# A third buffer pair for the experts' weights, memory lent between stages, and a shared term added on TensorE

## What is computed

```python
def channel_sublayer(x, shift, scale, gate, w_router, e_bias, w1, w3, w2, ws1, ws3, ws2, ln_g, ln_b):
    u = modulate(x, shift, scale)
    B, S, D = u.shape
    h = u.reshape(B * S, D)
    idx, wts = route(h, w_router, e_bias)
    y = (jax.nn.silu(h @ ws1) * (h @ ws3)) @ ws2 + routed_experts(h, idx, wts, w1, w3, w2)
    return post_norm(x, gate * y.reshape(B, S, D), ln_g, ln_b)
```

## Time and profile before

| what | value |
|---|---|
| median of three runs | 1322.1 us (1322.06 to 1329.15) |
| the profiled execution | 1323.07 us, of which the span 1321.3 us |
| mean granted TensorE clock | 0.917 |
| PE, DVE, ACT, POOL busy | 78%, 32%, 18%, 17% |
| read and written | 329.15 MB, 29.52 MB, 271 GB/s over the span |

### The profile page before, as it was taken

How to read it: one execution, slowest core, us unless ns; L and a number is a source line. 1 busy time by engine, 2 the same in 40 slices (tenths; PEclk the granted TensorE clock), 3 DMA queues, 4 the chain that set the end, 5 groups by cost and what they waited for, 6 DMA issues and landing times.

```text
span 1321.3 us, 23547 instructions
## 1 busy us (share of the span) xinstructions
PE 1033.8 (78%) x8385; PEld 657.7 (50%) x8386; DVE 427.7 (32%) x815; ACT 239.2 (18%) x478; POOL 218.1 (17%) x361
## 2 busy tenths in 40 slices
PE   4899899986576699983787788877877878766865
PEld 3888788875565344542344444444433444433432
DVE  4523324338843113874411111111111121101118
ACT  3222212336455000110110101010100111100100
POOL 0002102000100000201222222222231223212211
PEclk9899999996799799997799889899898998978988
DMA  9587666521063793075689699987999988899955
GB/s 350 173 298 256 223 236 216 184 95 48 1 226 112 274 272 115 32 301 201 215 291 386 229 382 395 370 326 272 408 375 387 328 303 299 308 398 404 396 220 216
DMA packets 97912, 347.52 MB, mean 263 GB/s; under 512 B 15057, under 2 KB 20225, under 8 KB 73146
## 3 DMA queue, kind: packets, MB, share of 16 engines
q1 hardware_dynamic: 81258, 311.56, 63.7%
q0 software_dynamic: 13856, 30.13, 6.9%
q10 hardware_dynamic: 2736, 4.98, 1.0%
HBM read 329.15 MB, written 29.52 MB: 271 GB/s over the span
## 4 chain that ended last, share of the span: by engine, by line
PE 27%; DMA 16%; issue 6%; DVE 2%; SPq 1%; ACT 0%; POOL 0%; POOLq 0%; DVEq 0%; ACTq 0%
PE PS L1771 8%; DMA hT<-h_rows,ixo 7%; DMA W<-w 7%; PE PS L1786 6%; PE PS L1802 4%; PE PS L1827 4%; PE PS L1841 2%; PE PS L1777 1%; DMA vec<-ln_b 1%; PE PS L1759 1%; PE PS L1817 1%; DVE hido L1893 0%; PE PS L1794 0%; DVE hid L1888 0%; DMA W<-expert_rows 0%
## 5 line engine op out<-in xcount | busy, mean ns | idle before, releaser
L1771 PE MATMUL PS<-W,XT 128*32 128x256 f32 x2048 | 130.0, 410 | 48.5 <-DMA W<-w 26.5
L1786 PE MATMUL PS<-W,XTo 128*64 128x256 f32 x1216 | 139.5, 381 | 0.0
L1771 PEld LDWEIGHTS PS<-W,XT 128*32 128x32 f32 x2048 | 80.1, 118 | 114.8 <-issue 90.6
L1786 PEld LDWEIGHTS PS<-W,XTo 128*64 128x64 f32 x1216 | 93.2, 137 | 44.0 <-issue 10.6
L1802 PE MATMUL PS<-W,hidTo 128*64 128x512 f32 x304 | 90.7, 722 | 16.3 <-DVE hidTo L1896 10.7
L431 DVE TENSOR_TENSOR w_lo<-raw,w_hi 128x2048 fp32r<-128x2048 f32 x26 | 59.5, 2288 | 126.1 <-ACT w_hi L371 126.1
L305 PE MATMUL PS<-w_hi,u_hi 128*128 128x512 f32 x240 | 94.4, 393 | 1.7 <-DVE w_lo L431 1.7
L305 PE MATMUL PS<-w_hi,u_lo 128*128 128x512 f32 x240 | 93.5, 389 | 0.0
L305 PE MATMUL PS<-w_lo,u_hi 128*128 128x512 f32 x240 | 93.4, 389 | 0.0
L1827 PE MATMUL PS<-W,hidT 128*32 128x512 f32 x512 | 72.1, 677 | 26.3 <-issue 24.3
L1856 ACT ACTIVATE sg<-PS 64x256 f32<-64x256 f32 x32 | 12.1, 378 | 346.9 <-PE PS L1771 346.9
(11 more groups left out here) (338 smaller groups left out, 1497.8 us busy)
## 6 DMA issues: line engine op xcount, KB each, us to landing
W<-w SPq DMA_DIRECT2D x192, 1024.0 KB, 13.9
raw<-w_in SPq DMA_DIRECT2D x26, 1024.0 KB, 9.2
oaT<-w_ada SPq DMA_DIRECT2D x8, 1536.0 KB, 8.6
W<-expert_rows SPq DMA_DIRECT2D x24, 512.0 KB, 12.5
obT<-w_ada SPq DMA_DIRECT2D x8, 512.0 KB, 8.9
kc<-cache_k_diff SPq DMA_DIRECT2D x8, 512.0 KB, 4.8
vc<-cache_v_diff SPq DMA_DIRECT2D x8, 512.0 KB, 3.5
Wa<-p_a SPq DMA_DIRECT2D x4, 1024.0 KB, 7.5
```

What stands on the lines that cost most here:

```text
L1771: mm = pe.matmul(PS[64 * h + 32 * c:64 * h + 32 * c + 32, UP_B + i, 0:F], XT[:, i, k, 32 * c:32 * c + 32], t.W13[:, 2 * i + c, h, k], star ...
L1786: mm = pe.matmul(PS[64 * h:64 * h + 64, XH_B, 0:F], XTo[:, k], t.W13[:, slot, h, k], start=k == 0, stop=k == KD - 1)
```

## The change

- The ring of weights has three pairs (`RING = 3`): pair n lies in place n % 3 and is refilled with pair n + 3. The third pair's memory is one tensor, `third`.
- Until the experts' stage, `third` is lent: to the router's state and to `MT` and `U2` in `projection_out`, to `ws2_sb`, `SL` and `CB` in `routing`. The one-hot tensor `oh` moves to `obT`. After pair 29, `third` holds `vec` and `diag`.
- The third pair is loaded at the start of `experts`, where `vec` was loaded. `vec` is now loaded behind all weight loads, once `yy_mm` counts 30 pairs.
- The loop has passes of six pairs: three pairs are written out, four passes, then five pairs.
- VectorE starts its pairs at once. `diag` is made after the last pair. The gate and `ALPHA` steps on `t.acc` are gone: TensorE multiplies `t.acc` by the identity into the sums of rows (six products of 512 columns), and `ALPHA * x` is joined by the last addition, for each of three tiles. The result is made in `t.X` in place of `t.acc`.

```diff
-        LOOPS = (PAIRS - 3) // PW
+        PERIOD, LOOPS = PW * RING, (PAIRS - RING - 5) // (PW * RING)
...
-            for n in range(PW):
-                body(n, n, 0, n)
-            with eng.Fori(1, LOOPS) as it:
-                for i in range(PW):
-                    body(it * PW + i, i, it, None)
-            for n in range(LOOPS * PW, PAIRS):
-                body(n, n % PW, n // PW, n)
+            for n in range(RING):
+                body(n, n % PW, n // PW, n % RING, n // RING, n)
+            with eng.Fori(0, LOOPS) as it:
+                for r in range(RING, RING + PERIOD):
+                    body(it * PERIOD + r, r % PW, it * RING + r // PW, r % RING, it * PW + r // RING, None)
+            for n in range(RING + LOOPS * PERIOD, PAIRS):
+                body(n, n % PW, n // PW, n % RING, n // RING, n)
...
-                if within(fixed, PW):
+                if within(fixed, RING):
                     sp.wait_ge(h_mm, n + 1)
...
-                        load_up(sp, t, expert_at(it + 1, 2 * i + c), 2 * i + c)
+                        load_up(sp, t, expert_at(it + 1 + i, 2 * (1 - i) + c), 2 * w + c)
                     sp.wait_ge(yy_mm, n + 1)
...
-                        load_down(sp, t, expert_at(it + 1, 2 * i + c), 2 * i + c)
-
+                        load_down(sp, t, expert_at(it + 1 + i, 2 * (1 - i) + c), 2 * w + c)
+
+            for c in range(2):
+                load_up(sp, t, expert_at(1, c), WB + c)
+            for c in range(2):
+                load_down(sp, t, expert_at(1, c), WB + c)
+            loops(sp, body)
+            sp.wait_ge(yy_mm, PAIRS - 2)
             t.load_mod(sp, vec, 5, vec_in)
             sp.dma_start(vec[:, 2], t.ln2_g.to_broadcast([P, D])).then_inc(vec_in, 16)
             sp.dma_start(vec[:, 3], t.ln2_b.to_broadcast([P, D])).then_inc(vec_in, 16)
-            loops(sp, body)
...
             loops(pe, body)
+            pe.wait_ge(yy_ev, PAIRS)
+            for n in range(NT):
+                for c in range(2):
+                    pe.matmul(PS[:, SUM_B[n] + c], t.ident[:, :], t.acc[:, n, CW * c:CW * c + CW], start=True, stop=False)
             pe.wait_ge(diag_done, 1)
...
             link = make_link(dve, dve_step)
-            dve.wait_ge(vec_in, 64)
+            loops(dve, body)
             for n in range(NT):
                 for k in range(OWN[n], TOPK):
                     ins = dve.tensor_scalar(diag[n][:, k - OWN[n]], t.ident[:, :], t.wts[:, n, k:k + 1], None, ALU.mult)
             ins.then_inc(diag_done, 1)
-            for n in range(NT):
-                a = t.acc[:, n]
-                link(dve.tensor_tensor(a, a, vec[:, n // 2], ALU.mult))
-                link(dve.scalar_tensor_tensor(a, t.X[:, n], ALPHA, a, ALU.mult, ALU.add))
-            loops(dve, body)
+            dve.wait_ge(vec_in, 64)
...
-                    link(dve.tensor_tensor(a, a, r, ALU.add))
+                    link(dve.scalar_tensor_tensor(a, a, ALPHA, r, ALU.mult, ALU.add))
```

More of the change, by code:

```diff
@@ L51 @@
 WB = 2 * PW
+RING = 3
 QC = {0: 0, 1: 4, 6: 8}
@@ L1351, in expert_at, with up_of, down_of @@
     return turn + E // WB * slot
+def up_of(t, i):
+    return t.W13[:, i] if i < WB else t.third_up[:, i - WB]
+def down_of(t, i):
+    return t.W2[:, i] if i < WB else t.third_down[:, i - WB]
 def load_up(sp, t, e, i):
[L1356 to L1357 removed]
+    sp.dma_start(up_of(t, i)[:, 0], of_expert(t.w1v, e)).then_inc(t.wup_in[i], 16)
+    sp.dma_start(up_of(t, i)[:, 1], of_expert(t.w3v, e)).then_inc(t.wup_in[i], 16)
 def load_down(sp, t, e, i):
[L1362 removed]
+    sp.dma_start(down_of(t, i), of_expert(t.w2v, e)).then_inc(t.wdown_in[i], 16)
 def routing(nc, t):
@@ L1379, in routing @@
         t8, i8, i8f = sb("t8", [P, NT, 8]), sb("i8", [P, NT, 8], U32), sb("i8f", [P, NT, 8])
-        oh = sb("oh", [P, NT, TOPK, E])
+        oh = t.obT[:, :, :].rearrange("p u q -> p (u q)").rearrange("p (n k e) -> p n k e", n=NT, k=TOPK)
         mask = sb("mask", [P, NT, E], F16)
@@ L1611, in experts @@
         OWN = (2, 2, 3)
-        diag, vec = [sb(f"diag{n}", [P, TOPK - OWN[n], P]) for n in range(NT)], sb("vec", [P, 4, D])
+        t.lent[0] = 0
+        vec, diag = t.lend("vec", [P, 4, D]), [t.lend(f"diag{n}", [P, TOPK - OWN[n], P]) for n in range(NT)]
         vec_in = sem("vec7_in")
@@ L1657, in _, with body @@
         def _(sp):
-            def body(n, i, it, fixed):
-                if within(fixed, PW):
+            def body(n, i, it, w, q, fixed):
+                if within(fixed, RING):
                     sp.wait_ge(h_mm, n + 1)
@@ L1771, in up @@
                             mm = pe.matmul(PS[64 * h + 32 * c:64 * h + 32 * c + 32, UP_B + i, 0:F], XT[:, i, k, 32 * c:32 * c + 32],
-                                           t.W13[:, 2 * i + c, h, k], start=k == 0, stop=k == KD - 1)
+                                           up_of(t, 2 * w + c)[:, h, k], start=k == 0, stop=k == KD - 1)
                 mm.then_inc(h_mm, 1)
@@ L1785, in step @@
                         for h in range(2):
-                            mm = pe.matmul(PS[64 * h:64 * h + 64, XH_B, 0:F], XTo[:, k], t.W13[:, slot, h, k], start=k == 0, stop=k == KD - 1)
+                            mm = pe.matmul(PS[64 * h:64 * h + 64, XH_B, 0:F], XTo[:, k], up_of(t, slot)[:, h, k], start=k == 0, stop=k == KD - 1)
                     mm.then_inc(o_h, 1)
@@ L1801, in step, with body @@
                         for h in range(2):
-                            mm = pe.matmul(PS[64 * h:64 * h + 64, XY_B], hidTo[:, j], t.W2[:, slot, j, CW * h:CW * h + CW], start=j == 0, stop=j == 1)
+                            mm = pe.matmul(PS[64 * h:64 * h + 64, XY_B], hidTo[:, j], down_of(t, slot)[:, j, CW * h:CW * h + CW], start=j == 0, stop=j == 1)
                     mm.then_inc(o_y, 1)
                 return step
-            def body(n, i, it, fixed):
+            def body(n, i, it, w, q, fixed):
                 first = extra_bounds(pe, n)
-                up(n, i, it)
+                up(n, i, w, q)
                 if within(fixed, 1):
@@ L1811, in body @@
                 for c in range(2):
-                    extra(pe, first[c], first[c + 1], extra_block(2 * i + c, it))
+                    extra(pe, first[c], first[c + 1], extra_block(2 * w + c, q))
                 pe.wait_ge(hid_done, n + 1)
@@ L1827, in body @@
                             mm = pe.matmul(PS[64 * h + 32 * c:64 * h + 32 * c + 32, Y_B], hidT[:, i, j, 32 * c:32 * c + 32],
-                                           t.W2[:, 2 * i + c, j, CW * h:CW * h + CW], start=j == 0, stop=j == 1)
+                                           down_of(t, 2 * w + c)[:, j, CW * h:CW * h + CW], start=j == 0, stop=j == 1)
                 mm.then_inc(yy_mm, 1)
@@ L1841, in _ @@
                         mm = pe.matmul(PS[:, SUM_B[n] + c], diag[n][:, k - OWN[n]], G[n][:, k, CW * c:CW * c + CW],
-                                       start=k == OWN[n], stop=k == TOPK - 1)
+                                       start=False, stop=k == TOPK - 1)
                 mm.then_inc(row_pe, 1)
@@ L1933, in _ @@
             for n in range(NT):
-                a, r, gate = t.acc[:, n], G[n][:, 0], vec[:, n // 2]
+                a, r, gate = t.X[:, n], G[n][:, 0], vec[:, n // 2]
                 summed = PS[:, SUM_B[n]:SUM_B[n] + 2].rearrange("p b x -> p (b x)")
@@ L2021, in streaming_layer @@
         t.ident_done = ctx.enter_context(nc.semaphore("ident_done"))
-        t.wup_in = [ctx.enter_context(nc.semaphore(f"wup_in{i}")) for i in range(WB)]
-        t.wdown_in = [ctx.enter_context(nc.semaphore(f"wdown_in{i}")) for i in range(WB)]
+        t.wup_in = [ctx.enter_context(nc.semaphore(f"wup_in{i}")) for i in range(2 * RING)]
+        t.wdown_in = [ctx.enter_context(nc.semaphore(f"wdown_in{i}")) for i in range(2 * RING)]
         t.phase_sems = []
@@ L2097, in streaming_layer, with lend @@
             t.wr_in = phase_semaphore("wr_in")
-            t.router = router_state(lambda n, shape, d=F32: scoped(ctx, n, shape, d))
+            third = scoped(ctx, "third", [P, 2 * (2 * KD * F + 2 * D)])
+            t.third_up = third[:, 0:4 * KD * F].rearrange("p (e h k f) -> p e h k f", e=2, h=2, k=KD)
+            t.third_down = third[:, 4 * KD * F:].rearrange("p (e j d) -> p e j d", e=2, j=2)
+            t.lent = [0]
+            def lend(name, shape, dtype=F32):
+                size = 1
+                for length in shape[1:]:
+                    size *= length
+                words = size // 2 if dtype == F16 else size
+                part = third[0:shape[0], t.lent[0]:t.lent[0] + words]
+                t.lent[0] += words
+                assert t.lent[0] <= third.shape[1], name
+                part = part if dtype == F32 else part.bitcast(dtype)
+                if len(shape) == 3:
+                    return part.rearrange("p (a b) -> p a b", a=shape[1])
+                if len(shape) == 4:
+                    return part.rearrange("p (a b c) -> p a b c", a=shape[1], b=shape[2])
+                return part
```

(3 more changed lines are left out.)

26 lines of the change are left out of this document (13 added, 13 removed).

## The result

The changed kernel takes 1330.28 us (median of 20 executions, 1324.59 to 1341.54) against 1322.43 for the kernel before: ratio 1.0055, 95% interval 1.0036 to 1.0074. The prediction was 1294, faster. So the change makes the kernel 0.6% slower, and the prediction was wrong by 36 us. The profiled execution took 1324.59 us with a span of 1322.6, 1.3 more than before.

The account below looks back on a forecast made before the run. Bound: the experts' chain through TensorE, stopping for DMAs (26.5 us weights, 28.7 rows). Sum: -6.8 - 1.7 - 29.7 + 9 + 3 - 1.5 = -27.7, from the median 1322.1 to 1294; range 1274 to 1304.

Parts of the forecast that it names:

- The loop of six pairs: Experts' loop: 5 us gained from fewer branches, 13.9 lost to code loading; net +9 us, between -5 and 41.
- code loading is worse: Third rival, in the loop: 1.43 us per packet gives 1326, chance 0.13; 2.5 per packet gives 1355, chance 0.05.
- Pair 0: Start of the experts' stage: with VectorE free, pair 0 takes 17.90 us in place of 24.73, a gain of 6.8.
- The first fetch: Start of the experts' stage: first row fetch lands in 9.5 us in place of 11.2; 1.7 gained, between 0 and 3.5.
- The waits for weights: Pairs 17 and 18 gain 9.3 us, pairs 24 to 30 gain 21.4; less 1 for small misses, 29.7.
- the second sum: Pairs 24 to 30: 103.22 us falls to a clean 81.83, a gain of 21.4.
- the first rival: Last eight pairs: weight supply binds at a rate below 410 GB/s; at 360, arrivals slip 11 us, 1305; chance 0.08.
- The vectors and the last scatter: After the last pair: `vec` transfers keep the queue busy, delaying last scatter and rows; +3 us, between 0 and 6.5.
- The end: After the loop: `diag` and identity products are hidden; a shorter TensorE pause keeps the clock up, -1.5 us, between -3 and 0.
- the second rival: Extra blocks: fetches of rows meet fuller queues and wait longer, 14 us more, 1308; chance 0.08.

Follow-up runs that it names:

- The loop alone: Kernel before, still two pairs of weight buffers, with pairs written as three, four passes of six, and five: 1341.76 us, ratio 1.0178.
- the straight kernel: Changed kernel with all 32 pairs written out, so that no branch goes back: 1308.55 us, ratio 0.9914.
- the short loop: Changed kernel with a loop of three pairs, rows, results and indices in three buffers, hidden rows in one: median 1300.5 us of 17 executions.
- the runs with one branch and none: Changed kernel with a loop of twelve pairs run twice: 1320.69 us, ratio 0.9973; and with all 32 pairs written out: 1308.55 us, ratio 0.9914.
- the ends alone: Kernel before with only the change's vectors, `diag` and shared rows' addition, two pairs of buffers and loop of two kept: 1312.19 us, ratio 0.9899.
- the rows first: Ring of three with a loop of three pairs, third pair of weights requested only after the first three row fetches land: median 1294.75 us of 11.

## Why the prediction was wrong, step by step

**The loop of six pairs: the step that failed.** The prediction held that code loading was possible, gave it 27 packets of 0.24 us and three branches of 2.5, and took +9 with 12 branches saved, "as most packets before passed unseen". Measured between the changed kernel and the ring with a loop of three: 1330.28 - 1300.5 = 29.8 us. That loop has eight passes and so seven branches back, which save 5 x 0.55 against twelve, so the term was about +27 (an estimate, as these two kernels differ in more than the loop). The loop alone on the kernel before costs 23. The mechanism was named, its price was put in the wrong place. A branch back costs about three times what I gave it: its stop (7.50, 7.76, 4.99) and the cold products behind it (6.4 - 3.66, which the sum forgot), some 28.6 us on the timeline, of which 18.6 by the straight kernel reach the end. The packets themselves don't cost 0.24 each; the rest of the cost falls on single jumps of 2 to 4 us, nearly all where a skipped extra block brings TensorE to code that is not there yet. From the straight kernel to the short loop, where these stops are gone as well, it is about another 8 us. The prediction took the one visible stop of 1.43 us, spread it over six packets and so averaged a price away that falls on single jumps.

The rival "code loading is worse" gave 1326 for this and had 0.13. That it came near is luck in part: it priced each of 27 packets at 1.43 us, and the runs with one branch and none show a price per branch and per jump. Its argument for itself, that pairs without extra blocks outrun the loading, was the right one (though not over "a packet and a half", which is a whole pair's code by the earlier trace rows). Its argument against itself, pair 30, was a poor one: pair 30 has an extra block, so it runs through its code and jumps over less.

By the Trainium skill (Runtime: NRT & Kernel Launch, Instruction fetch mechanics) a branch to code that isn't in memory waits for its DMA, while crossing from block to block in sequence is mostly hidden. The runs agree on both: 5.0 to 9.9 us at branches back, and 32 packets in the straight kernel with nine stops of 1.7 to 4.1 us, nearly all where extra blocks were jumped over. With the 128 KiB in blocks of 16, eight blocks, that the prediction quoted from there, six packets that stay and nine that don't are in keeping.

**Pair 0: right.** Predicted 6.8 us, measured 24.73 - 18.19 = 6.5, and 7.1 with the ends alone. The wait for `hido` fell from 4.96 to 0.56:

```profile
639.42 0.31 PE L1810 MATMUL PS<-ident,hido 64*128 64x64 f32 x2 [0.56 <-DVE hido L1913]
```

**The first fetch: within its bounds.** Predicted 1.7 between 0 and 3.5; from the fetch's issue to the first up product it is 627.63 - 614.17 = 13.46 against 14.58, 1.1 gained. The remaining 1.6 of the -2.75 is the stage's earlier beginning in this execution (614.17 against 615.80), which no step explains. That the six weight DMAs hold the rows up was assumed. The run with the rows first shows it, where they are only asked for later: 624.45 - 616.84 = 7.6 us from issue to product, and 7.5 (625.02 - 617.51) with the ends alone, which have none of them.

**The waits for weights: right place, too large.** Predicted 29.7. In the kernel with the short loop and the rows first, where no code hides them, pairs 17 and 18 take 36.91 us and pairs 24 to 30 take 90.20: 6.6 and 13.0, 19.6 together. In the first place no weights are waited for any more; pair 18 takes 28.0 us where the sum took the 25.66 of another pair with two extra blocks for its clean length, so the term was mis-sized. The rest of the second sum is the first rival, supply. In that kernel pair 24 starts at 1130.91 and pair 28's products at 1170.88, 40.0 later, where the prediction had weights at 31.7 and need at 34.3 (windows as in rows 7, then the product):

```profile
1130.90:1170.90 40.00, 26.14 (x364) 14.74 (x365) 6.34 (x12) 3.86 (x8) 10.47 (x17) 0.97 1.01 374
```

```profile
1170.88 5.67 PE L1799 MATMUL PS<-W,XT 128*32 128x256 f32 x64 [7.04 <-DMA W<-w]
```

The DMA engines are busy all the time (share 1.01) and move 374 GB/s, not the 410 of rows 7. The bytes that the prediction counted were too few as well: 374 GB/s for 40 us is 15.0 MB, where 31.7 us at 410 are 13.0. The rate is worth 13.0 / 0.374 - 31.7 = 3.1 us of the 8.3 between 31.7 and 40.0, the bytes the other 5.2. That supply is the cause is read from these rows; no run took bytes away to test it. The 358 GB/s that the Trainium skill (DMA: Bandwidth & Descriptors, Where 436 GB/s comes from) names as a bound were exceeded in these stretches too (374, and 410 in rows 7), so the bound doesn't hold here.

**The vectors and the last scatter: no cost.** Predicted 3, between 0 and 6.5. In the chain that ended last the scatter of the changed kernel takes what it took before:

```profile
1269.31 2.63 DMA expert_rows<-obT,dx
```

The queues were nearly empty by then: from 1264 to 1269 the DMA engines are busy 17% of the time and move 61 GB/s, so the vectors had come through.

**The end: right in sum.** The identity products run in the pause, and the clock behind it no longer falls; from 1270 to 1280 it is 1.00 where it was 0.51:

```profile
1268.52 5.42 PE L1855 MATMUL PS<-oaT,ident 128*128 128x512 f32 x12 [0.80 <-DVE obT L1931]
```

```profile
1270.00:1280.00 10.00, 7.04 (x17) 2.78 (x16) 1.79 (x10) 1.15 (x1) 0.30 (x1) 1.00 0.73 270
```

The products of sums run at full speed, but behind the first they now wait twice for rows (0.54 us at 1278.85, 0.57 at 1281.41). Of 2.8 us 1.2 are gained; 1.5 was predicted. That half was a guess between two ends, and it fell near by luck: the clock stayed up all through, and the rows took the rest.

**Fetched rows: the second rival didn't happen.** 28.9 us after 28.7. In the runs with the short loop it is 31.0 to 33.1, 2 to 4 us more.

**The sum again.** With 27 in place of 9 for the loop, 19.6 in place of 29.7 for the weights, 0 in place of 3 for the scatter and the small terms as measured (-6.5, -1.1, -1.2): -1.4, where the span grew by 1.3 and the medians by 8. The step between these numbers stays open: the profiled execution was the fastest of its 20, so its stops may have been the shortest.

## What to carry to other kernels

A longer period of a ring is paid in code: before a loop body is lengthened, compare its size with bodies that the trace shows to stay, and price each branch back at a whole stop and the cold products behind it (6 to 8 us of device time together here), not at an average over packets. Where a ring of three met something of period two, it was cheaper here to make the other buffers three than the loop six. And transfers that are not needed for 30 us can be asked for behind the small fetch that is needed at once: its wait fell by 4.6 us, though how much of that reaches the end is open.

## What the runs showed of the hardware that was not expected

A loop body of four pairs ran without loading, one of six loaded itself anew in every pass, and the step between them was sharp: 4 instruction packets, all in the first pass, against 37 in the same 420 us. A branch back to absent code stopped TensorE for 5.0 to 9.9 us, several times the stop of 1.43 us that the kernel before had shown. And issuing a weight transfer, 0.3 to 0.5 us as a rule, took SyncE up to 5 us where many were under way (timeline of SyncE, ring with the short loop and the rows first):

```profile
1153.01 0.40 SPq L1365 DMA_DIRECT2D third<-w  x1
...
1155.77 2.41 SPq L1365 DMA_DIRECT2D third<-w  x1
...
1168.24 4.97 SPq L1365 DMA_DIRECT2D W<-w  x1
```

No loss is seen from it there, as the DMA engines were busy all the time (share 1.01 from 1130.9 to 1170.9); no run tests it.
